# A mixture-of-experts router fed from the unnormalised residual, its top four picked for both token tiles together

## The reference, cut to what matters

```python
x1 = x + g1 * rms_norm(m, norm_post_mix)
h  = rms_norm(x1, norm_pre_ffn) * (1 + sc2) + sh2
logits = h @ w_router + b_router               # 256 x 32
top_v, top_e = top_k(logits, 4)
gates = softmax(top_v)
f   = sum over the four experts e of gates * mlp_e(h)
out = x1 + g2 * rms_norm(f, norm_post_ffn)
```

## Time and profile before

| what | us |
|---|---|
| median of 3 runs | 1467.84 |
| lowest and highest of them | 1461.21, 1473.31 |
| the profiled execution: time | 1461.84 |
| the same execution: span of the trace | 1460.0 |
| busy in it: PE, DVE, ACT, POOL | 1270.1, 484.3, 248.9, 119.0 |
| DMA over the span | 458.88 MB, mean 314 GB/s |

### The profile page before, as it was taken

How to read it: one execution, slowest core, us unless ns; L and a number is a source line. 1 busy time by engine, 2 the same in 40 slices (tenths; PEclk the granted TensorE clock), 3 DMA queues, 4 the chain that set the end, 5 groups by cost and what they waited for, 6 DMA issues and landing times.

```text
span 1460.0 us, 27228 instructions
## 1 busy us (share of the span) xinstructions
PE 1270.1 (87%) x11208; PEld 586.6 (40%) x11209; DVE 484.3 (33%) x1052; ACT 248.9 (17%) x485; POOL 119.0 (8%) x160
## 2 busy tenths in 40 slices
PE   5999999357885799998989898987999999999995
PEld 1555445356653333433333333332433333433432
DVE  1246335742777522212221222211321321322323
ACT  2321522023512111111111111100100010100101
POOL 0201410453503000000000000000000000000000
PEclk9999999656996799999999999998999999999998
DMA  9516273000155499999999999999999699969993
GB/s 363 232 36 223 74 275 113 2 33 5 62 222 211 199 427 427 428 427 428 428 428 428 428 428 428 428 425 428 426 429 427 266 427 427 429 296 402 428 427 151
DMA packets 47824, 458.88 MB, mean 314 GB/s; under 512 B 4369, under 2 KB 4753, under 8 KB 22673
## 3 DMA queue, kind: packets, MB, share of 16 engines
q1 hardware_dynamic: 47762, 457.96, 75.5%
HBM read 456.31 MB, written 1.05 MB: 313 GB/s over the span
## 4 chain that ended last, share of the span: by engine, by line
PE 43%; DMA 28%; DVE 5%; issue 4%; ACT 2%; POOL 1%; ACTq 0%; POOLq 0%; DVEq 0%
DMA arena<-in_w_up 28%; PE bank L1119 21%; PE bank L1148 8%; PE bank L1091 3%; PE bank L1082 2%; PE bank L1025 2%; ACT arena L1479 1%; PE bank L1112 1%; PE bank L757 1%; PE bank L775 1%; PE bank L1143 1%; PE bank L830 0%; POOL arena L2253 0%; PE bank L700 0%; PE bank L869 0%
## 5 line engine op out<-in xcount | busy, mean ns | idle before, releaser
L1119 PE MATMUL bank<-arena 128*64 128x512 f32 x2176 | 483.3, 597 | 33.4 <-DMA arena<-in_w_up 19.1
L1119 PEld LDWEIGHTS bank<-arena 128*64 128x64 f32 x2176 | 155.0, 137 | 343.0 <-issue 269.6
L1148 PE MATMUL bank<-arena 128*64 128x512 f32 x1088 | 239.4, 592 | 0.0
L2121 DVE TENSOR_SCALAR arena<-bank 128x512 f32<-128x512 f32 x34 | 23.6, 693 | 394.6 <-PE bank L1119 394.6
L1148 PEld LDWEIGHTS bank<-arena 128*64 128x64 f32 x1088 | 78.5, 136 | 138.1 <-issue 135.7
L631 PE MATMUL bank<-arena 128*128 128x512 f32 (+1 forms) x320 | 122.4, 539 | 0.4 <-DMA arena<-in_wfm 0.4
L2102 DVE TENSOR_TENSOR arena<-arena,bank 128x512 f32<-128x512 f32 x140 | 86.6, 683 | 6.0 <-PE bank L1091 6.0
L631 PEld LDWEIGHTS bank<-arena 128*128 128x128 f32 x320 | 60.6, 192 | 60.3 <-issue 54.0
L1082 PEld LDWEIGHTS bank<-arena 128*128 128x128 bf16 x1680 | 60.3, 118 | 27.0 <-DVE arena L2125 25.8
L1091 PE MATMUL bank<-arena 64*128 64x512 f32 x280 | 69.6, 615 | 0.9 <-ACT arena L1481 0.9
L1082 PE MATMUL bank<-arena 128*128 128x64 bf16 x1680 | 64.2, 199 | 1.1 <-DVE arena L2044 1.1
(11 more groups left out here) (328 smaller groups left out, 1096.7 us busy)
## 6 DMA issues: line engine op xcount, KB each, us to landing
arena<-in_w_gate SPq DMA_DIRECT2D x64, 2048.0 KB, 20.2
arena<-in_w_up SPq DMA_DIRECT2D x64, 2048.0 KB, 21.8
arena<-in_w_down SPq DMA_DIRECT2D x64, 2048.0 KB, 20.3
arena<-in_w_ada SPq DMA_DIRECT2D x12, 2048.0 KB, 8.9
arena<-in_wfm SPq DMA_DIRECT2D x20, 512.0 KB, 6.8
arena<-in_wz SPq DMA_DIRECT2D x2, 2048.0 KB, 20.0
arena<-in_w_out SPq DMA_DIRECT2D x2, 2048.0 KB, 8.8
arena<-in_x SPq DMA_DIRECT2D x2, 1024.0 KB, 9.9
```

Source lines behind the costliest of these rows:

```text
L1119: last = mm(ps[m][64 * c_:64 * c_ + 64, :], xcT[:, k, :], ring[:, 2 * h_ + m, k % 4, 512 * c_:512 * c_ + 512], start=False, stop=(k == KT ...
L1148: last = mm(ps[2][64 * c_:64 * c_ + 64, :], hidT[:, k % 4, 64 * (k // 4):64 * (k // 4) + 64], ring[:, 4 + h_, k % 4, 512 * c_:512 * c_ + 5 ...
L2121: v.tensor_scalar(hid[:, 0], ps[0][:, :], LIMIT, None, ALU.min).then_inc(*L.mark("a"))
```

## The change

The router no longer reads `h`. With r(t) the reciprocal root of a token's mean square of x1, `logits = r(t) * (x1 @ (rows1 * w_router)) + (sh2 @ w_router + b_router)`. So:

- PE turns the two rows `rows[:, 1]` and `rows[:, 3]` into columns (16 matmuls of 128 x 128 weights by 2 columns, after the first `mixed` of stage "ssd"); ACT copies them out (`rcols`); POOL multiplies `w_router` by the first (`wrs`); PE multiplies the second, broadcast, with `w_router` (8 matmuls at the head of "route"), ACT copies that and POOL adds the bias (`b_all`).
- PE transposes x1 instead of h, and does tile 0's logits ahead of tile 1's transposes. DVE does both `x1` before either `h` is made (`second_factor` is the small reciprocal root, split from `second_norm`). The junk output of ACT's squares goes to another area.
- On DVE one instruction for each tile applies the factor and adds `b_all`. The indices of both tiles go through one compare and one sum for `chosen`; the weighting and `gate` come after the selection matrices (`weigh`).
- The bf16 parts: ACT rounds both tiles (`rounded`), the first subtraction is DVE's for tile 0 and POOL's for tile 1, the second subtraction of both writes bf16 directly, on DVE, after `chosen`. Before, there were three roundings and two subtractions for each tile.

```diff
@@ -338,8 +338,11 @@
         nmax = route(2, 1)
-        oneh = route(2, 32)
-        rtmp = route(2, 32)
+        oneh = route(2, TOP_K, 32)
+        weighed = route(2, TOP_K, 32)
+        wrs = route(KT, 32)
+        rcols = route(2, KT)
+        b_all = route(32)
         chosen = route(2, 32)
@@ -1029,6 +1032,12 @@
             mixed(0)
+            for j, row in enumerate((1, 3)):
+                for k in range(KT):
+                    at_ = 2 * (KT * j + k)
+                    last = mm(ps[4][:, at_:at_ + 2], rows[:, row, 128 * k:128 * k + 128], ident[:, 0:2], start=True, stop=True)
+            last.then_inc(*L.mark("rcols"))
             pe.wait_ge(*L.at("in", "wout0", 1))
@@ -1053,17 +1062,23 @@
             L.stage("route")
+            pe.wait_ge(*L.at("in", "wr", 1))
+            pe.wait_ge(*L.at("act", "rcols"))
+            for k in range(KT):
+                last = mm(ps[1][:, 256:288], rcols[:, 1, k:k + 1].broadcast_to([P, P]), wr[:, k, :], start=(k == 0), stop=(k == KT - 1))
+            last.then_inc(*L.mark("b_all"))
             for t in range(2):
-                pe.wait_ge(*L.at("dve", "h", t))
+                pe.wait_ge(*L.at("dve", "x1", t))
                 for k in range(KT):
-                    last = nc.tensor.transpose(unit(ps[6 - 2 * t + k // 4], k % 4), hm[:, t, 128 * k:128 * k + 128], ident)
+                    last = nc.tensor.transpose(unit(ps[6 - 2 * t + k // 4], k % 4), xin[:, t, 128 * k:128 * k + 128], ident)
                 last.then_inc(*L.mark("hT", t))
-            pe.wait_ge(*L.at("in", "wr", 1))
-            for t in range(2):
+                pe.wait_ge(*L.at("pool", "wrs"))
                 pe.wait_ge(*L.at("act", "hT", t))
                 for k in range(KT):
-                    last = mm(ps[2 * t][:, 0:32], hT[:, k, 128 * t:128 * t + 128], wr[:, k, :],
+                    last = mm(ps[2 * t][:, 0:32], hT[:, k, 128 * t:128 * t + 128], wrs[:, k, :],
                               start=(k == 0), stop=(k == KT - 1))
@@ -1092,7 +1107,8 @@
             pe.wait_ge(*L.at("dve", "Sb1"))
-            pe.wait_ge(*L.at("pool", "hparts"))
+            pe.wait_ge(*L.at("act", "hparts", 1))
+            pe.wait_ge(*L.at("dve", "hparts", 1))
             pe.wait_ge(*L.at("pool", "zeros"))
@@ -1414,6 +1430,8 @@
             mixed_out(0, 0)
+            act.wait_ge(*L.at("pe", "rcols"))
+            f(rcols, view(ps[4][:, 0:32], 2, KT, 2)[:, :, :, 0], ACT.Copy).then_inc(*L.mark("rcols"))
             y_root(0)
@@ -1436,7 +1454,7 @@
                 act.wait_ge(*L.own())
-                f(area("hT", 0, D), xin[:, t], ACT.Square, accum_out=newt[:, t, 5:6]).then_inc(*L.mark())
+                f(mix[:, t], xin[:, t], ACT.Square, accum_out=newt[:, t, 5:6]).then_inc(*L.mark())
                 act.wait_ge(*L.own())
@@ -1447,19 +1465,39 @@
             m_root(1)
+            def turned(t):
+                act.wait_ge(*L.at("pe", "hT", t))
+                for c_ in range(2):
+                    f(hT[:, 4 * c_:4 * c_ + 4, 128 * t:128 * t + 128], view(ps[6 - 2 * t + c_][:, :], 4, 128), ACT.Copy).then_inc(*L.mark("hT", t))
+            turned(0)
+            act.wait_ge(*L.at("pe", "b_all"))
+            f(b_all, ps[1][:, 256:288], ACT.Copy).then_inc(*L.mark("b_all"))
             x1_root(1)
+            turned(1)
             act.wait_ge(*L.own())
...
             prepare(ACT.Exp)
-            for t in range(2):
-                act.wait_ge(*L.at("pe", "hT", t))
-                act.wait_ge(*L.own())
-                for c_ in range(2):
-                    f(hT[:, 4 * c_:4 * c_ + 4, 128 * t:128 * t + 128], view(ps[6 - 2 * t + c_][:, :], 4, 128), ACT.Copy).then_inc(*L.mark("hT", t))
-            for t in range(2):
+            def rounded(s_, t):
+                act.wait_ge(*(L.at("dve", "h", t) if s_ == 0 else L.at("pool" if t else "dve", "rest", t)))
+                f(hparts[:, s_, t], hm[:, t] if s_ == 0 else x1[:, t], ACT.Copy).then_inc(*L.mark("hparts", s_, t) if s_ == 0 else L.mark("hparts", t))
+            def chances(t):
                 act.wait_ge(*L.at("dve", "nmax", t))
                 f(gexp[:, t], top[:, t, 0:4], ACT.Exp, bias=nmax[:, t], accum_out=gsum[:, t]).then_inc(*L.mark("gexp", t))
+            rounded(0, 0)
+            rounded(0, 1)
+            rounded(1, 0)
+            for t in range(2):
+                chances(t)
+            rounded(1, 1)
             act.wait_ge(*L.at("pe", "gather1"))
@@ -1990,10 +2028,13 @@
                 v.tensor_tensor(xin[:, t], mix[:, t], xin[:, t], ALU.add).then_inc(*L.mark("x1", t))
-            def second_norm(t):
+            def second_factor(t):
                 dve.wait_ge(*L.at("act", "r2", t))
                 refine_of(5, slice(t, t + 1))
+            def second_norm(t):
                 v.scalar_tensor_tensor(out=hm[:, t], in0=xin[:, t], scalar=newt[:, t, 12:13], in1=rows[:, 1], op0=ALU.mult, op1=ALU.mult).then_inc(*L.mark())
@@ -2002,42 +2043,54 @@
             m_ahead(1)
+            second_factor(0)
+            first_residual(1)
             second_norm(0)
-            first_residual(1)
+            second_factor(1)
             second_norm(1)
...
             L.stage("route")
-            for s_ in range(3):
-                dve.wait_ge(*L.own())
-                v.tensor_copy(hparts[:, s_, 0], hm[:, 0] if s_ == 0 else x1[:, 0]).then_inc(*L.mark())
-                if s_ < 2:
-                    dve.wait_ge(*L.own())
-                    v.tensor_tensor(x1[:, 0], hm[:, 0] if s_ == 0 else x1[:, 0], hparts[:, s_, 0], ALU.subtract).then_inc(*L.mark())
-            for t in range(2):
+            def best(t):
                 dve.wait_ge(*L.at("pe", "logit", t))
-                v.tensor_tensor(logit[:, t], ps[2 * t][:, 0:32], b_rt, ALU.add).then_inc(*L.mark())
+                dve.wait_ge(*L.at("pool", "b_all"))
+                v.scalar_tensor_tensor(out=logit[:, t], in0=ps[2 * t][:, 0:32], scalar=newt[:, t, 12:13], in1=b_all, op0=ALU.mult, op1=ALU.add).then_inc(*L.mark())
                 dve.wait_ge(*L.own())
...
                 v.tensor_scalar(nmax[:, t], top[:, t, 0:1], -1.0, None, ALU.mult).then_inc(*L.mark("nmax", t))
-                dve.wait_ge(*L.own())
-                v.tensor_copy(topf[:, t], topi[:, t]).then_inc(*L.mark())
-                dve.wait_ge(*L.at("act", "gexp", t))
-                v.reciprocal(gsum[:, t], gsum[:, t]).then_inc(*L.mark())
-                dve.wait_ge(*L.own())
-                v.tensor_scalar(gexp[:, t], gexp[:, t], gsum[:, t], None, ALU.mult).then_inc(*L.mark())
-                dve.wait_ge(*L.own())
-                for k in range(TOP_K):
-                    dst = (chosen[:, t], gate[:, t]) if k == 0 else (oneh[:, t], rtmp[:, t])
-                    dve.wait_ge(*L.own())
-                    v.tensor_scalar(dst[0], const("iota32"), topf[:, t, k:k + 1], None, ALU.is_equal).then_inc(*L.mark())
-                    v.tensor_scalar(dst[1], const("iota32"), topf[:, t, k:k + 1], gexp[:, t, k:k + 1], ALU.is_equal, ALU.mult).then_inc(*L.mark())
-                    if k:
-                        dve.wait_ge(*L.own())
-                        v.tensor_tensor(chosen[:, t], chosen[:, t], oneh[:, t], ALU.add).then_inc(*L.mark("chosen"))
-                        v.tensor_tensor(gate[:, t], gate[:, t], rtmp[:, t], ALU.add).then_inc(*L.mark())
+            best(0)
+            dve.wait_ge(*L.at("act", "hparts", 0, 0))
+            v.tensor_tensor(x1[:, 0], hm[:, 0], hparts[:, 0, 0], ALU.subtract).then_inc(*L.mark("rest", 0))
+            best(1)
+            dve.wait_ge(*L.own())
+            v.tensor_copy(topf, topi).then_inc(*L.mark())
+            dve.wait_ge(*L.own())
+            v.tensor_tensor(oneh, const("iota32").unsqueeze(1).unsqueeze(1).broadcast_to([P, 2, TOP_K, 32]),
+                            topf[:, :, 0:TOP_K].unsqueeze(3).broadcast_to([P, 2, TOP_K, 32]), ALU.is_equal).then_inc(*L.mark())
+            dve.wait_ge(*L.own())
+            v.tensor_reduce(chosen, oneh.rearrange("p t k e -> p t e k"), AX.X, ALU.add).then_inc(*L.mark("chosen"))
+            for t in range(2):
+                dve.wait_ge(*L.at("act", "hparts", t))
+                v.tensor_tensor(hparts[:, 2, t], x1[:, t], hparts[:, 1, t], ALU.subtract).then_inc(*L.mark("hparts", t))
+            def weigh():
+                for t in range(2):
+                    dve.wait_ge(*L.at("act", "gexp", t))
+                v.reciprocal(gsum, gsum).then_inc(*L.mark())
+                dve.wait_ge(*L.own())
+                v.tensor_tensor(gexp, gexp, gsum.broadcast_to([P, 2, TOP_K]), ALU.mult).then_inc(*L.mark())
+                dve.wait_ge(*L.own())
+                v.tensor_tensor(weighed, oneh, gexp.unsqueeze(3).broadcast_to([P, 2, TOP_K, 32]), ALU.mult).then_inc(*L.mark())
+                dve.wait_ge(*L.own())
+                v.tensor_reduce(gate, weighed.rearrange("p t k e -> p t e k"), AX.X, ALU.add).then_inc(*L.mark())
+                dve.wait_ge(*L.own())
             def choose(slots, step):
```

(17 more changed lines are left out.)

## The result

The changed kernel took 1455.14 us (median of 20 runs, 1448.74 to 1466.09), the kernel before 1465.64 beside it (20 runs). The ratio is 0.9925, with an interval of 0.9906 to 0.9943: 11.0 us less (8.3 to 13.8). A second set on another chip gave 1454.41 and 0.9917 [0.9892, 0.9941]. The forecast was 1454.4 and a ratio of 0.9909, 13.4 us less than the 1467.84 of the three runs that it started from.

The account below looks back on a forecast made before the run. The bound was the stream of expert weights, whose start hangs on the first gather. The route's steps put the gather at 468.4, plus 1.0 for the late projection: 469.4 against 482.78, 13.4 us less, 1454.4; range 1445 to 1463.

Parts of the forecast that it names:

- Before the route: Mixer's end: 32 column-matmul records take 3.6 us, projection starts 1.1 late; loss 1.0 us, between nothing and 2.
- rival 2: PE's clock stays up through the projection despite narrow matmuls: gather 1.4 us sooner, 16.7 less, 1451.1; chance 0.1.
- x1(1) first: DVE makes x1(1) before h(0): x1(1) stands at 453.2, 2.4 us earlier; h(1) at 459.4, against 460.7.
- PE in the route: PE's `b_all`, transposes and logits: tile 0's logits end at 455.8, tile 1's at 462.4, 7.0 us earlier.
- ACT: Exp table load and small activation take 1.5 us, to 460.4; roundings 1.1 each, done at 461.5 and 462.6.
- DVE's new wait: In the route, DVE waits 1.3 us for ACT's rounding of tile 0 before its subtraction.
- DVE's small work: Route: index copy 0.2 us, compare 0.63, sum 0.46; `chosen` at 464.8 against 479.3, 14.5 us earlier.
- The parts: bf16 parts end last: POOL's subtraction 2.4 us, DVE's last two 1.25 each, to 467.4; counts covered, gather at 468.4.
- Rival 1: DVE and POOL still hinder each other, subtractions 1.94 and 2.86 us: gather at 471.4, 11.4 less, 1456.4; chance 0.17.
- Behind the gather: Weighing (1.6 us) ahead of the table, written 7.1 behind the gather's start; SP needs it at 9.8, 2.7 us cover.
- rival 3: SP needs 4.3 us to read the table: expert 1's first issue 1.6 late, 11.8 less, 1456.0; chance 0.08.
- Sum: First gather at 468.4 + 1.0 = 469.4 against 482.78, so 13.4 us less at the end.

Follow-up runs that it names:

- after: First profiled trace of the changed kernel, all parts in; median 1455.14 us, ratio 0.9925 of the kernel before.
- e11: The changed kernel unaltered, run and profiled again on another chip; 1454.41 us, ratio 0.9917 of the kernel before.
- e4: Changed kernel with PE's transposes of tile 1 put ahead of tile 0's logits; 1456.60 us, ratio 0.9926 of the kernel before.
- e7: Changed kernel with the router's narrow matmuls made 128 columns wide by repeated values; 1453.96 us, ratio 0.9905 of the kernel before.
- e6: Changed kernel with the weighing moved from ahead of the table's write to behind it; one execution, 1464.19 us.
- e1: Changed kernel with the router reading h again, without column matmuls, h(0) made before x1(1); 1460.91 us, ratio 0.9959 of the kernel before.
- e2: Changed kernel with the bf16 parts again on two engines, DVE for tile 0, POOL for tile 1; 1463.21 us, ratio 0.9964 of the kernel before.
- e3: Kernel before with only both tiles' best four together and the weighing behind the selection matrices; 1461.11 us, ratio 0.9968 of the kernel before.
- e5: Changed kernel with the index copy done by ACT instead of DVE; one execution, 1456.16 us.
- e9: Changed kernel with the edits of e4, e5, e6 and e7, plus five unread full-width matmuls between logits and counts; 1453.06 us, ratio 0.989.
- e10: e9 with the weighing back ahead of the table; one execution, 1461.02 us.
- B: Part of the change: the best four of both tiles taken together; alone on the kernel before it is e3, ratio 0.9968.
- C: Part of the change: the three bf16 parts on three engines; undone in e2, ratio 0.9964 of the kernel before.
- A: Part of the change: the norm folded into the router's weights, with the order it allows; undone in e1, ratio 0.9959 of the kernel before.

## Why the prediction was right, step by step

The predicted instants are moved by the 1.53 us that the mark lies later in the trace of after, and include the 1.0 of the late projection.

*Before the route.* 32 narrow records, 3.6 us forecast, 3.63 measured; the projection 1.02 behind the point where DVE had been ready (1.1 forecast) and its end 0.93 later against the mark (1.0 forecast). **But this was one of two outcomes.** In e11 the clock did not fall and the end came 0.76 sooner than before. I gave that 0.1, as rival 2; with narrow records it came in three traces of six. The gather was then 15.0 us earlier, not 16.7. That the profiled execution fell on the side of my main case is luck.

*x1(1) first.* x1(1) ends at 455.68 (455.7 forecast), h(1) at 461.81 (461.9).

*PE in the route.* Logits of tile 0 end at 458.90 (458.3), of tile 1 at 465.54 (464.9): 0.6 late. Part of it is the copies that came in a row: PE waits 1.27 us for ACT each time.

*ACT.* The load and the activation behind it took 1.49 us (461.81 to 463.30), with nothing between the two; 1.5 was forecast. The Trainium skill, ScalarE: Activation LUTs, "What ACT_TABLE_LOAD costs", counts 2.7 with a drain; the trace does not agree, and the measurement decides.

*DVE's new wait.* 1.61 us, against 1.3. In e4 to e7 and in e11, where the first logits ran at full clock, it is gone.

*DVE's small work.* **This is where the sum was off.** I counted the index copy at 0.2 us. It took 1.67, until POOL's subtraction and two memsets were done. The compare (0.43 for 0.63) and the sum (0.59 for 0.46) cancel. `chosen` came at 469.19 against 467.3. The hold is there in each trace in which the copy of both tiles starts beside POOL's subtraction, and absent where POOL has finished:

| trace | index copy, us | POOL meanwhile |
|---|---|---|
| after, e4, e6, e7, e11 | 1.67, 1.83, 1.82, 1.82, 1.82 | busy; the copy ends 0.03 to 0.04 behind its last memset |
| e1, e2, e3 | 0.18, 0.18, 0.24 | done, or done just after it starts |
| e5 (on ACT) | 0.20 | busy |

A busy POOL alone doesn't do it. In the kernel before, the 8-column copy of tile 0 took 0.21 us, from the end of a rounding on POOL into its memsets, the second of which ended only at 471.80. How long POOL must still be busy, and with what, no run separates.

```profile
469.68 1.38 POOL L2345 CAST arena<-arena 128x1024 bf16<-128x1024 f32 x1
...
470.87 0.21 DVE L2026 CAST arena<-arena 128x8 f32<-128x8 uint32 x1
...
471.27 0.52 POOL L2352 MEMSET arena<- 128x512 f32 x1
```

*The parts.* POOL's subtraction took 2.09 (2.4 forecast) and ended at 467.37, against 467.5. The last subtractions ended at 471.46 where 469.9 was forecast, since the copy held them. The counts ended at 471.59, so the two were even, and only nearly as said. The gather came at 472.70 against 470.9: 1.8 late, of which the copy is 1.5.

*Rival 1* gives a gather at 472.9 on this scale, almost the measured one, but for another reason: the three subtractions took 1.23 and 1.18 each, not 1.94, and POOL 2.09, not 2.86 (DVE's first subtraction overlapped POOL's by 0.24 us only, its last two not at all; in e4, e6, e7 and e9, where more of it did, POOL took 2.7). That engines get into each other's way was right, the instruction that paid was not the one named.

*Behind the gather.* The table was written 7.05 us behind (7.1 forecast). The issue followed 8.75 behind, not 9.8: the clock rose early, 2.7 us behind the gather's start (7.3 before), expert 0's first piece was done at 480.65, and then SP waited for the table after all, 479.75 + 1.70 = 481.45. In e7 it is the same 1.70. In the twelve other traces the issue comes 0.18 to 0.19 us behind PE's last matmul with the piece, in after and e7 0.80 and 0.79. So rival 3 was a real mechanism with a wrong price: SP needs 1.7 us from the table's write to the issue, not 4.3, and it costs 0.6, only where PE is back at full clock early. e6, e9 and e10, at half clock for most of the piece, show the issue 9.8, 10.2 and 10.0 behind the gather with tables that differ by 1.6.

*Sum.* Two errors nearly cancel: 1.8 us lost at the gather, 1.0 won behind it. At the issue it is 12.7 in the profiled executions, against 13.4. In the medians it is 11.0 (8.3 to 13.8). That the time itself came out 0.7 us from the forecast is partly luck: the three runs that I subtracted from had a median of 1467.84, the kernel before took 1465.64 beside the changed one, and the two misses, 2.2 us in the start and 2.9 in the difference of the medians (10.5 for 13.4), nearly cancel. The mechanism held up to the gather, but for the tie with the counts; the mis-sized terms are the index copy (0.2 for 1.67) and the distance from the gather to the issue (9.8 for 8.75).

*The clock and the narrow records.* Rows 7 and 8 had spoken for a fall with narrow records on a busy PE, and the two traces of the changed kernel bear it out in part. In after PE is busy 1.00 in the stretch from 420 to 421, and the granted clock goes there from 1.00 (2.4 GHz) to 0.50 (1.2 GHz): the mean of 0.90 puts it at 420.8. In the logits it stays at 0.50 under a busy PE. In e11 the same stream of work kept 1.00 through the projection. The Trainium skill, TensorE: Matmul & The Clock Gate, "Part 1: The HAM clock gate", goes by how busy PE has been recently; by that alone the fall at 420.8 would not have come. What decides between the two outcomes, no run here settles.

*Parts of the gain.* They don't add up as separate sums. Counted from the kernel before, B alone brings the gather 6.4 us forward (e3), B with C 7.8 (e1), B with A 8.2 (e2, which had the better clock), and all three 11.6, or 15.0 in e11. So on top of B, C alone adds 1.4 and A alone at most 1.8, but both together 5.2 to 8.6. With only one of them the other's wait stays: in e1 DVE waits for the logits, which end at 54.70, in e2 for its own splitting of tile 0.

## What to carry to other kernels

Where the end hangs on a stream of transfers, measure every edit at the stream's first issue and not at the end: here the mark scattered by 15 us between traces and the remainder behind the issue by 0.7. When work is spread over a third engine, look again at the small instructions of the others: a copy of 16 columns cost more than the 1024-column subtraction ahead of it. And a step that is off the path by a microsecond at one clock can be on it at the other, so read the cover of each wait at both.

## What the runs showed of the hardware

- A DVE copy of 16 columns within SBUF that began beside POOL's subtraction ended 0.03 to 0.04 us behind POOL's second memset in five traces (1.67 to 1.83 us, for 0.2), while DVE's MAX8, FIND_INDEX8 and operations of 32 columns with one input from PSUM went through beside the same POOL subtraction in their usual 0.2 to 0.25. An 8-column copy that began 0.19 us before the end of a POOL rounding was not held by the memsets (0.21, kernel before).
- The other way round, POOL's add of 32 columns ended 0.11 us behind the DVE operation of 1024 columns beside which it began, in each of the eleven traces that have it: it took 1.23 us in after, where that operation had just begun, and 0.42 in e4, where it was about to end. From the timeline of after:

```profile
455.60 1.28 DVE L2038 SCALAR_TENSOR_TENSOR arena<-arena 128x1024 f32<-128x1024 f32 x1
...
455.76 1.23 POOL L2400 TENSOR_TENSOR arena<-arena 128x32 f32<-128x32 f32 x1
```

- ACT's roundings of 1024 columns weren't slowed by POOL: 1.99 for two with POOL idle, 1.06 for one beside its subtraction.
- f32 matmuls of 2, 32 and 128 columns on a 128x128 weight cost nearly the same here: 3.63 us for 32 records, 1.94 for 16 and 2.04 for 16, all at full clock, so 0.11, 0.12 and 0.13 each.
- The same program fell to half clock in the projection in one execution and not in another, with 3.4 us between them at the gather.
- From DVE's write of the index table to SP's first issue that takes its index from it, 1.70 us passed in after and in e7, the two traces in which SP waited for the table and not for PE.
